# Triangular sums in a state-space scan, and attention with its values stationary, in a two-layer hybrid transformer kernel

## What is computed

```
def diff_attend(q, k, v, lam):
    s = einsum('bqhmd,bkhmd->bhmqk', q, k) * (DA_QK ** -0.5)
    p = softmax(s, axis=-1)
    a = p[:, :, 0] - lam * p[:, :, 1]
    return einsum('bhqk,bkhv->bqhv', a, v)          # then rms_norm per head, * subln_g * (1 - lam_init)

def ssd_chunked_scan(xh, dt, a, bm, cm, h0):        # per chunk of 128, both directions
    a_cum = cumsum(dt_c * a, axis=2)
    seg = a_cum[:, :, :, None, :] - a_cum[:, :, None, :, :]
    decay = exp(where(lower, seg, -inf))
    scores = einsum('bcihn,bcjhn->bcijh', c_c, b_c) * decay * dt_c[:, :, None, :, :]
    y_diag = einsum('bcijh,bcjhp->bcihp', scores, x_c)
```

## Time and profile before

| | us |
|---|---|
| median of three runs | 1417.57 |
| lowest and highest | 1416.66, 1420.8 |
| span of the profiled execution | 1417.9 |
| PE busy in it | 1172.4 |
| DVE, ACT, POOL busy | 463.5, 266.9, 122.1 |
| moved by DMA | 344.03 MB |

### The profile page before, as it was taken

How to read it: one execution, slowest core, us unless ns; L and a number is a source line. 1 busy time by engine, 2 the same in 40 slices (tenths; PEclk the granted TensorE clock), 3 DMA queues, 4 the chain that set the end, 5 groups by cost and what they waited for, 6 DMA issues and landing times.

```text
span 1417.9 us, 15930 instructions
## 1 busy us (share of the span) xinstructions
PE 1172.4 (83%) x6032; PEld 567.1 (40%) x6032; DVE 463.5 (33%) x1121; ACT 266.9 (19%) x592; POOL 122.1 (9%) x107
## 2 busy tenths in 40 slices
PE   5899978878989599999985499986799699995553
PEld 2363433444654333333332447432468333332222
DVE  5111456764742611111101421357663511110003
ACT  1220101223530411111101322001251311110002
POOL 2000031820000010000000200033200100000001
PEclk9999999979899799999998699997689799997776
DMA  9622106739996389999999401006003689999972
GB/s 337 242 86 93 60 0 261 289 131 412 374 353 274 140 326 372 389 390 395 395 399 397 187 4 56 0 0 237 0 1 119 252 313 385 388 410 413 407 327 93
DMA packets 86997, 344.03 MB, mean 243 GB/s; under 512 B 6918, under 2 KB 42187, under 8 KB 64395
## 3 DMA queue, kind: packets, MB, share of 16 engines
q1 hardware_dynamic: 67728, 309.68, 56.5%
q10 hardware_dynamic: 15195, 19.86, 4.1%
q0 software_dynamic: 4000, 13.49, 2.7%
HBM read 300.92 MB, written 42.07 MB: 242 GB/s over the span
## 4 chain that ended last, share of the span: by engine, by line
PE 61%; DMA 20%; DVE 11%; ACT 3%; issue 2%; SPq 1%; POOL 1%; ACTq 0%; POOLq 0%; DVEq 0%
PE ps L901 13%; PE ps L503 12%; DMA ring<-in_exp_w_up 10%; PE ps L924 6%; PE ps L791 6%; PE ps L512 5%; PE ps L446 4%; DMA ring<-in_w_mod 3%; DMA slots<-arena 2%; PE ps L468 2%; DMA arena<-in_exp_w_up 2%; PE ps L688 2%; PE ps L770 2%; PE ps L668 2%; PE ps L740 1%
## 5 line engine op out<-in xcount | busy, mean ns | idle before, releaser
L901 PE MATMUL ps<-ring,arena 128*32 128x256 f32 (+1 forms) x1344 | 197.8, 534 | 45.1 <-DMA ring<-in_exp_w_up 45.1
L503 PE MATMUL ps<-u,ring 128*128 128x512 f32 (+1 forms) x416 | 168.0, 564 | 9.5 <-ACT u L1743 4.0
L446 PE MATMUL ps<-cst,arena 128*128 128x128 f32 x558 | 110.3, 318 | 65.7 <-DVE arena L1445 33.0
L446 PEld LDWEIGHTS ps<-cst,arena 128*128 128x128 f32 x558 | 70.2, 160 | 172.0 <-issue 81.5
L901 PEld LDWEIGHTS ps<-ring,arena 128*32 128x32 f32 (+1 forms) x1344 | 71.3, 136 | 154.4 <-issue 146.5
L1601 DVE TENSOR_TENSOR arena<-arena,ps 128x128 f32<-128x128 f32 (+1 forms) x59 | 27.3, 503 | 317.3 <-ACT arena L1903 317.3
L503 PEld LDWEIGHTS ps<-u,ring 128*128 128x128 f32 x416 | 80.0, 194 | 94.9 <-issue 90.1
L901 PE MATMUL ps<-arena 128*64 128x512 f32 (+1 forms) x544 | 82.2, 528 | 17.6 <-DMA arena<-in_exp_w_up 17.6
L924 PE MATMUL ps<-arena 128*32 128x256 f32 (+1 forms) x672 | 94.4, 485 | 1.6 <-ACT arena L1912 1.6
L791 PE MATMUL ps<-u,ring 128*128 128x512 f32 (+1 forms) x256 | 83.6, 487 | 2.3 <-DVE h L1426 1.3
L512 PE MATMUL ps<-ring,u 128*128 128x256 f32 (+1 forms) x224 | 76.6, 502 | 7.7 <-DVE arena L1245 7.7
(11 more groups left out here) (291 smaller groups left out, 1221.9 us busy)
## 6 DMA issues: line engine op xcount, KB each, us to landing
ring<-in_w_mod SPq DMA_DIRECT2D x24, 2048.0 KB, 10.9
ring<-in_exp_w_gate SPq DMA_DIRECT2D x22, 2048.0 KB, 18.6
ring<-in_exp_w_up SPq DMA_DIRECT2D x22, 2048.0 KB, 23.0
arena<-in_exp_w_down SPq DMA_DIRECT2D x22, 2048.0 KB, 20.1
slots<-zeros SPq DMA_DIRECT2D x4, 6144.0 KB, 41.9
arena<-in_exp_w_gate SPq DMA_DIRECT2D x10, 2048.0 KB, 20.7
u<-in_exp_w_down SPq DMA_DIRECT2D x10, 2048.0 KB, 19.7
arena<-in_exp_w_up SPq DMA_DIRECT2D x10, 2048.0 KB, 26.7
```

The costliest lines, as they stand in the source:

```text
L446: return nc.tensor.transpose(dst, src, ident[0:n, 0:n])
L503: last = nc.tensor.matmul(bank[row:row + width, 0:T - c0], w[:, k, n:n + width], u[:, k, c0:T], start=(k == 0), stop=(k == KT - 1))
L901: last = nc.tensor.matmul(ps[n * part:n * part + n, 2 + b % 2, 0:2 * width].rearrange("p (s n) -> p s n", s=2), x_k, pair[:, :, a:a + widt ...
```

## The change

1. **Scan sums.** The sum runs over a strict triangle (`strict[d]`, made by two subtractions in `latents_up`, in the then free first columns of `wuq`) in place of ones. The result is the segment sum itself, which is not above 0 where it is used; the masked products set the rest to 0. The clamp goes. ACT reads banks 2 and 3 directly, and a cast waits for `decay_exp` in place of the clamp.
2. **Who does it.** `rows` goes from POOL to ACT, eight activations with a scale per partition for each direction. `weights` goes from POOL to DVE, one 128x1024 product for each direction.
3. **Where.** The masked products, casts and weights of tile 0 (and the products and casts of tile 1) go into `rotate`. Layer 0's seven modulation parts are put behind the outputs of a tile (`SCAN_MODS`).
4. **Attention.** Units alternate da, ml. Da scores have banks 2 and 3, ml scores bank 4. The score scale goes into the evacuation of q (DVE), the maximum is negated by its own instruction. Ml probabilities are scaled on DVE before they are transposed. Transposes run three units behind the scores (two before). For each two heads of a kind the values are stationary (64 columns each) and the transposed probabilities stream, 128 columns; the two heads use the two column halves of the array. The heads come out with features on partitions, so they aren't transposed again: ACT squares them, one matmul with block ones sums the squares, ACT takes the root, and DVE places them in one instruction.

The core of the diff:

```diff
-SCAN_MODS = (1, 1, 1)
+SCAN_MODS = ((1, 2), (0, 0))
-LAG_OUT, LAG_NORM, LAG_TURN, LAG_PLACE = 7, 8, 9, 10
+LAG_TURN, LAG_PV, LAG_SQUARE, LAG_MEAN, LAG_ROOT, LAG_ML, LAG_DA = 3, 3, 10, 10, 11, 11, 12
...
-            for t in range(0 if layer == 0 else NCTX // P, TT) for kind in ("da", "ml") for hh in range(DA_H)]
+            for t in range(0 if layer == 0 else NCTX // P, TT) for hh in range(DA_H) for kind in ("da", "ml")]
...
+                masked_products(l, 0)
+                cast_rows(l, 0, 0)
                 for m in range(4):
+                    if m == 2:
+                        cast_rows(l, 0, 1)
...
+                masked_products(l, 1)
+                for d in range(2):
+                    cast_rows(l, 1, d)
                 read_back(f"kr{l}")
...
                 if n >= 1:
-                    pe.wait_ge(S("decay_clamped"), 2 * tiles_before(l) + n)
+                    pe.wait_ge(S("decay_exp"), 2 * tiles_before(l) + n)
                 for b in range(2):
-                    last = nc.tensor.matmul(ps[:, 2 + b, :], ones[:, :],
+                    last = nc.tensor.matmul(ps[:, 2 + b, :], strict[d],
...
                     if i + 1 < len(tiles):
-                        cast_rows(i + 1, 1)
-                        spare(SCAN_MODS[1])
+                        spare(SCAN_MODS[l][0])
                     if i + 2 < len(tiles):
-                        scores(i + 2)
-                        cast_rows(i + 2, 0)
-                        spare(SCAN_MODS[2])
+                        masked_products(l, i + 2)
+                        cast_rows(l, i + 2, 0)
+                        spare(SCAN_MODS[l][1])
+                        cast_rows(l, i + 2, 1)
...
                         for k in range(nk // P):
-                            last = nc.tensor.matmul(ps[:, g % 2, 64 * hh:64 * hh + 64], probs_t[:, n % 2, k, :],
-                                                    v[:, k, 64 * hh:64 * hh + 64], start=(k == 0),
-                                                    stop=(k == nk // P - 1))
+                            for unit in (n - 2, n):
+                                hh = units[unit][2]
+                                r, c = 64 * (hh % 2), P * (hh // 2)
+                                last = nc.tensor.matmul(heads_of(kind)[r:r + 64, c:c + P],
+                                                        v[:, k, 64 * hh:64 * hh + 64], probs_t[:, unit % 4, k, :],
+                                                        start=(k == 0), stop=(k == nk // P - 1),
+                                                        tile_position=(0, r))
...
+            def weights(l, i, d):
+                dve.wait_ge(S("decay_exp"), 2 * tiles_before(l) + 2 * i + d + 1)
+                own_read()
+                part = ews[i % 2][d].rearrange("p (g h) i -> p g h i", g=2)
+                tt(part, part, gms[i % 2][:, d].unsqueeze(2).to_broadcast([P, 2, 4, P]), ALU.mult).then_inc(
+                    S("w_ready"), 1)
...
-                        link(v.tensor_reduce(mx[:, s, 0:nm], ps[:, pair:pair + nm, 0:nk], AX.X, ALU.max))
-                        ts(nb[:, s, 0:nm], mx[:, s, 0:nm], -(DA_SCALE if kind == "da" else MLA_SCALE), None,
-                           ALU.mult).then_inc(S("max_ready"), 1)
+                        v.tensor_reduce(nb[:, s, 0:nm], scores_of(kind)[:, :, 0:nk], AX.X, ALU.max,
+                                        negate=True).then_inc(S("max_ready"), 1)
...
+                def rows(i, d):
+                    at_dt = 32 * d + 8 * (FIRST_T[l] + i)
+                    for hh in range(SSD_H):
+                        last = a(ews[i % 2][d][:, hh, :], tri[d], ACT.Identity, scale=sc[:, 2, at_dt + hh:at_dt + hh + 1])
+                    last.then_inc(S("rows_built"), 1)
+                def decays(i, d):
+                    act.wait_ge(S("rows_cast"), 2 * tiles_before(l) + 2 * i + d + 1)
+                    a(ews[i % 2][d], ps[:, 2:4, :].rearrange("p b (h i) -> p (b h) i", i=P), ACT.Exp).then_inc(
+                        S("decay_exp"), 1)
```

More of the change, by code:

```diff
@@ L715, in attention @@
                 units = attention_units(l)
-                before, groups_before = units0 * l, units0 // DA_H * l
+                before = units0 * l
                 pe.wait_ge(S("roped"), l + 1)
-                for s in range(len(units) - DA_H + LAG_TURN + 1):
+                for s in range(len(units) - HEAD_UNITS + LAG_MEAN + 1):
                     if s == 1:
@@ L1281, in scan_tiles @@
                     if i + 1 < len(tiles):
-                        clamp(i + 1, 1)
+                        for d in range(2):
+                            weights(l, i + 1, d)
                     dve.wait_ge(S("y_summed"), tiles_before(l) + i + 1)
@@ L1358, in attention @@
+                            link(ts(second, second, rr[:, n, 1:2], None, ALU.mult))
+                            stt(first, first, rr[:, n, 0:1], second, ALU.mult, ALU.add).then_inc(S("mixed"), 1)
                         else:
+                            first = probs_of(n)[:, 0, 0:nk]
                             link(v.reciprocal(rr[:, n, 0:1], rs[:, n, 0:1]))
+                            ts(first, first, rr[:, n, 0:1], None, ALU.mult).then_inc(S("mixed"), 1)
                     spare(mod_in_attention(l, s))
[L1361 to L1364 removed]
@@ L1622, in _ @@
             v.memset(small[:, 20:21], EPS)
+            for l in range(DEPTH):
+                v.memset(small[:, 21 + l:22 + l], EPS / (1.0 - lam_init(l)) ** 2)
             link(v.memset(cond[:, :, :], 0.0))
```

358 lines of the change are left out of this document (162 added, 196 removed).

## The result

| | before | changed |
|---|---|---|
| median (runs) | 1417.92 us (4) | 1409.52 us (4) |
| lowest and highest | 1416.66, 1420.8 | 1407.11, 1412.62 |
| span of the profiled execution | 1417.9 | 1405.3 |

The ratio is 0.9932, 95% interval 0.991 to 0.9954: faster by 9.6 us. The forecast was 1391.5, range 1374 to 1406; the time lies outside it, and the gain is little more than a third of the 26 us forecast. The profiled execution of the change (1407.11 us, span 1405.3) is the fastest of its four, so its trace shows some 3 us more gain than the ratio.

What follows compares the result with a forecast made beforehand. PE, busy 83% of the span, was taken as the bound. Gains of 9.3 + 2.3 + 12 + 3.3 less 1.1 make 25.8 us; 1417.9 - 25.8 = 1392.1, likeliest 1391.5, range 1374 to 1406.

Steps and rivals of the forecast that it cites:

- So DVE becomes the bound at full clock, 17.6 us a tile: Attention, units of 512 keys: DVE's work of 4.4 us a pair of da and ml bounds it, against 22 us a tile before.
- the round trip of the da banks: Attention: scores 1.1, maximum 1.2, two exponents 1.45 and signals 0.2 make 4.0 us, below DVE's 4.4 a pair.
- the forecast's own signs of being wrong: Rows over 0.4 us each, value passes over 0.1 us, or PEclk 0.50 through a whole tile more than now.
- Tail: End of attention, behind the last scores: transposes, copy, values, square, sum, root, placing take 8.65 us, against 7.3 before.
- Layer 0, scan: PE stays the bound; less idle time and half clock, minus two new waits: gain 9.3 us, or 5 with ACT or DVE on the path.
- The rival with ACT on the scan's path: Scan, both layers: rows at 0.41 us and Silu table loads hold the casts, half the scan's gain goes, 1403; chance 0.10.
- Layer 0, modulation: DMA covers what shorter units would save; no gain of its own, the stretch moves up by 9.3 us with the scan.
- Layer 1, scan: Tile 0 starts earlier, tile 1 follows sooner and at a better clock: 16.3 us, less 4.3, gain 12, bounds 5 and 17.
- Tile 0 starts 8.5 us earlier: Layer 1's scan: tile 0's weights are made inside the rotation, so its outputs start 8.5 us earlier than at 990.66.
- Layer 1, attention: Third unit's scores to output projection: seven pairs 30.8, tail 8.65, half clock 8.1, 47.5 us against 50.75; gain 3.3.
- Values no cheaper: Attention: half-width value matmuls between whole-array transposes cost 1.7 us for two units, 15 of 25.8 us are left, 1403; chance 0.15.
- The slower rival: Attention: PE idles a little in every pair, the clock falls to 1.2 GHz and stays, 1436 us; chance 0.05.

Runs made afterwards that it cites:

- The experiment with tile 0 first: The change with tile 0's outputs ahead of tile 1's second cast, and DVE's weights for that direction behind tile 0's sums: 1407.72 us, ratio 0.9912.

## Why the prediction was wrong

**The step that failed** is "So DVE becomes the bound at full clock, 17.6 us a tile", 4.4 a pair. Its terms were about right: the value matmuls cost 1.02 us for two units (369.35 to 370.37; forecast 0.9, and 1.7 by the rival), DVE's work 4.1 a pair. But it took the largest of the engines' sums for the period of a pair. The one loop that it had, the round trip of the da banks at 4.0, ended at the exponents. The measured period is that of loops that go on through the engines' queues: 4.64 us through the mixing and 6.01 through ACT's copy and PE's values, in turn, 5.33 in the mean. The order shown ahead of the prediction had it: values right behind the transposes and scores of the same step. With the values one step later the pair takes 4.54 and layer 0's attention 45.4 us, where the forecast had 45.5 at full clock. The range was wrong with it: no rival had the attention slower than today at full clock. By the stretches of the traces this step cost 5.9 and 3.5 us of the forecast gain in the two attentions; layer 1's scan is short of it by 4.2, and the start, by chance, by 2.1. With the values one step later the time is 1382.6, 9 us below the forecast: its attentions are 5.8 and 6.4 us shorter than forecast, nearly all of the 13.8 us that the forecast had allowed there for half clock.

Of the forecast's own signs of being wrong none came (rows 0.30 us, value passes 0.064, no further tile at half clock). What did show it was a sign of being right that stayed away: eight units of 512 keys take 21.3 us at full clock, at 5.33 a pair, not 18 to 19, and DVE has gaps.

**Tail.** 8.65 forecast. In the change 10.7 us (last scores done at 395.8, projection at 406.47), because copies and values wait in turn, and because a group of values and one of transposes run at 1.2 GHz there (1.98 and 1.12 us and not 1.09 and 0.66); 8.2 in the version with the later values.

**Layer 0, scan.** Gain 9.3 forecast, 9.8 measured: 5.3 us of idle time (6.05 forecast) and 4.5 of work at a higher clock (3.3 forecast), so two errors of about 1 us cancel. PE was the bound, with waits of 0.3 to 1.2 us in the scan's tiles. The price of ACT's rows, 0.32 each, was measured at 0.30 (16 in 4.78 us). The rival with ACT on the scan's path didn't occur.

**Layer 0, modulation.** From the first to the last chunk of the attention 37.4 us before, 37.4 in the change, and 37.2 to 37.8 in every experiment, whatever the attention's order: the transfers bound it, as forecast, and the stretch moved with the scan. DMA's share rose to 1.03.

**Layer 1, scan.** Gain 12 forecast, 7.8 measured. The distance from tile 0's to tile 1's outputs was right (8.2 forecast, 8.31), and so was the half clock in tile 1 (9.6 us). The wrong term is "Tile 0 starts 8.5 us earlier": by its distance from the states it starts 4.2 us earlier. (The forecast's three terms also add up to 16.7 and not 16.3.) The 982 us was reached only since layer 1 began 3.6 us earlier; PE did tile 1's casts first, one of them at 1.2 GHz (3.78 us). The experiment with tile 0 first gives back 4.8 us of scan.

**Layer 1, attention.** 3.3 forecast, nothing measured: the same 5.33 a pair (1023.77 to 1034.43 for two), with less time at 1.2 GHz (PEclk 0.81 from 1002 to 1042, 0.50 before). The better clock hid what the loop cost.

**Rivals.** Values no cheaper: refuted, 0.064 us a pass and no idle time between these matmuls and the whole-array transposes behind them (370.37 in the change). The Trainium skill has the rule (page TensorEngine Tiling (Array Packing), section Key Properties) that a change of tiling mode drains TensorE. The traces show little of it. Behind da scores the values start after 1.06 us (368.29 to 369.35), as the transposes did before; behind ml scores they start after 0.95 (362.62 to 363.57 with the later values), where transposes start after 0.86 in the change (370.87 to 371.73). The slower rival had the right engine, PE idle in each pair, but looked for its price in the clock; the price was idle time at full clock.

**Small costs.** 1.1 forecast, 1.3 measured (0.66 a layer).

## What to carry to other kernels

When a loop is staged by lags, don't take the largest sum of an engine as its period: write down each engine's order for one period and follow the loop through every instruction that stands ahead in a queue. Two stages of one unit on PE, between which the data pass another engine's queue, need a step between them; here one such step was worth 25 us, and one too few between scores and transposes cost 52, over half of it by the clock. And try a part of a change with the others present: the strict sum and its place lost the whole gain of the scan when either was undone, and the order of the casts paid only once fillers held the clock.

## What the runs showed of the hardware

- With matmuls that nobody reads in its waits, TensorE kept 2.4 GHz through tile 1's outputs at the end of layer 1's scan (PEclk 0.91 and 0.94 from 970 to 1000 us, 0.54 without), at no cost in time. Making the scan shorter without them lengthened the half-clock stretch (34 us and not 27) and gave the gain back.
- The same kind of DVE instruction (128x512) took 0.69 us beside POOL with one input in PSUM, and 1.55 and 2.16 us with both in SBUF.
- Two heads in column halves, with 128 columns streaming, run at 0.064 us a pass, and whole-array transposes follow without a gap.
